# The residual gate of a mixture-of-experts block, multiplied into the expert rows while they leave PSUM

## The chip, the core and the metric

One core of one Trainium2 chip runs the whole program. The metric is the device time of one execution in microseconds (us); lower is better. Engines: TensorE (PE; its weight loads are PEld), VectorE (DVE), ScalarE (ACT), GpSimd (POOL) and SyncE (SP). SP and POOL issue nearly all DMAs here; POOL alone issues the indirect ones.

## The reference, cut to what matters

Two layers of a hybrid attention and mixture-of-experts model over 640 tokens of 1024 numbers: 128 prompt tokens and 512 latents. All values are 32-bit floats. Each layer ends so:

```
sh1, sc1, gt1, sh2, sc2, gt2 = modulation(cond, w_mod, b_mod)   # cond differs for prompt and latents
...
h2 = rms_norm(x, g_norm2) * (1 + sc2) + sh2
x = x + gt2 * moe(h2, w_router, b_router, w_gate, w_up, w_down)
```

In `moe` each token picks one group of experts and then its two best of the 16 experts, with weights w1 + w2 = 1:

```
for e in range(16):
    hid = silu(h @ w_gate[e]) * (h @ w_up[e])       # 256 wide
    out = out + combine[..., e:e + 1] * (hid @ w_down[e])
```

The gate gt2 is a row of 1024 numbers, one for the prompt tokens and one for the latents. The change is about where gt2 is multiplied.

## The kernel before

**Tiles of rows.** Tokens are held as five row tiles (NT = 5) of 128; tile 0 is the prompt. In the expert stage the 1280 pairs of token and expert are sorted into 18 expert tiles (MOE_TILES) of 128 slots. A "full" tile serves one expert, a "pair" tile two experts with 64 slots each. The order `SCHED` is: full, full, pair, full, pair, ... full, full, pair, so from tile 2 on the even tiles up to 14 are pairs, and tile 17 is one. Full tiles from tile 3 on are "split": their operands are cut into a high and a low part, and three matmuls take the place of one. ScalarE makes the high part (`moe_hi`), VectorE the low part (`moe_lo`, L1715; `x_lo`, L1720).

**One expert tile n.** POOL gathers the token rows (`rows`, L795) and, for a pair, the weights (`gu_a`, `gu_b`, `dn_a`, `dn_b`, L804 and L811); SP loads the weights of full tiles. TensorE, in this order within iteration n: `gate_up(n)` into PSUM bank 0, the transposes of the next tile's rows (L2197), `down(n - 1)` into banks 2 and 3, `hid_transposes(n)` (L2271). It goes on to `gate_up(n + 1)`, which waits for `hid(n)` on VectorE and, for a split tile, for `x_lo(n + 1)`. ScalarE does silu of one half of bank 0 (L1187), VectorE multiplies it with the other half into `hid` (L1758).

**The rows' way out.** `ys(n)` copies banks 2 and 3 out to `ysb[n % 2]`, a row of 1024 per slot, times the slot's weight `w_slot`: columns 0 to 511 on ScalarE (L1178), 512 to 1023 on VectorE (L1732). It waits for `down(n)` and, from tile 2 on, for the store of tile n - 2 from the same buffer (`y_stored`). Both engines do `ys(n - 1)` in iteration n, VectorE behind `hid(n)` and `x_lo(n + 1)`. POOL then scatters the row tile to `ye_d` in HBM (`store_rows`, L830). These stores stand in POOL's queue between the gathers of later tiles. `down(n)` on TensorE waits for `ys(n - 1)`.

**Rows of a layer put together.** When all stores have landed, SP loads for each row tile t the two rows of each token, `Y1[t]` and `Y2[t]`, two loads of 512 KB (`load_back`, L610). Before that, `rows_return` has loaded x (L598) and, behind its first tile, the gate as `gt` (two loads of 512 KB, broadcast over the partitions, L601). VectorE does three operations on 128x1024 per row tile, each behind the one before: Y1 += Y2 (`mix_rows`, L1357), Y1 *= gt (`gate_rows`, L1361), x += Y1 (`add_rows`, L1365). After layer 0 they are interleaved with the head of layer 1: square and root on ScalarE (L954, L958), scale (L962), transposes on TensorE (L1802), modulation shared by ScalarE (L968) and VectorE (`head_half`, L1337), high part on ScalarE (L972, L974). After layer 1 nothing but the three operations and the stores to `y_out` (L672) is left.

Of the kernel before, what the change touches and what calls it, by code (L numbers as in the profile page):

```python
# [137 lines left out]
def program(nc, w_stream, w_gu, w_dn, x_in, c_cols, params, b_mod2, vecs, g_norm2, da_kc, da_vc, na_kc, na_vc, na_bias,  # L138
# [3 lines left out]
    with ctx:  # L142
# [56 lines left out]
        tok = at("tok", [P, 2 * NT], F32)  # L199
        junk_off = top[0]  # L200
# [59 lines left out]
        ecmp = at("ecmp", [P, N_FULL + N_HALF, N_EXP], F32, 92)  # L260
        rc_f = at("rc_f", [P, NRC], F32, 92)
# [215 lines left out]
        y_act = Signal("y_act", MOE_TILES)  # L477
        y_dve = Signal("y_dve", MOE_TILES)
        y_stored = [Signal(f"y_stored{b}", half[b], 0, 16) for b in range(2)]
        gathered = [Signal(f"gathered{t}", 5 if t == 0 else 3, 0, 16) for t in range(NT)]  # L480
# [73 lines left out]
        def _(sp):  # L554
# [9 lines left out]
            for l in range(DEPTH):  # L564
# [26 lines left out]
                def rows_return(l):  # L591
# [4 lines left out]
                    sp.wait_ge(mod_stored.sem, mod_stored.at(l, 3))  # L596
                    for t in range(NT):
                        sp.dma_start(x[:, t, :], x_spill[:, t, :]).then_inc(gathered[t].sem, 16)  # L598
                        if t == 0:
                            for cond in range(2):  # L600
                                sp.dma_start(gt[:, cond, :], mod_d[l, cond, 5 * D:6 * D].partition_broadcast(P)  # L601
                                             ).then_inc(gathered[0].sem, 16)
# [39 lines left out]
                head_pair(3)  # L642

# [33 lines left out]
        def _(po):  # L677
# [17 lines left out]
            for l in range(DEPTH):  # L695
# [131 lines left out]
                def store_rows(n):  # L827
                    po.wait_ge(y_act.sem, y_act.at(l, n))
# [51 lines left out]
        def _(act):  # L880
# [4 lines left out]
            for l in range(DEPTH):  # L885
# [284 lines left out]
                def ys(n):  # L1170

                    act.wait_ge(*down_done(l, n))
                    if n >= 2:
                        act.wait_ge(y_stored[n % 2].sem, y_stored[n % 2].at(l, n // 2 - 1))
                    if n == 0:
                        act.wait_ge(ws_ready.sem, ws_ready.at(l, 0))
                    c = XD_COL[n]
                    act.activation(ysb[n % 2][:, 0:512], ps[:, 2, :], ACT.Copy, scale=w_slot[:, c:c + 1]).then_inc(y_act.sem, 1)  # L1178

                x_in_act(0)  # L1180
                for n in range(MOE_TILES):
# [10 lines left out]
                    if n >= 1:  # L1192
                        ys(n - 1)
# [8 lines left out]
                ys(MOE_TILES - 1)  # L1202
# [7 lines left out]
        def _(dve):  # L1210
# [9 lines left out]
            for l in range(DEPTH):  # L1220
# [134 lines left out]
                def mix_rows(l, t):  # L1355
                    dve.wait_ge(gathered[t].sem, gathered[t].at(l, gathered[t].n - 1))
                    after(chained(dve.tensor_tensor(Y1[t][:], Y1[t][:], Y2[t][:], ALU.add)))  # L1357

                def gate_rows(l, t):
                    mix_rows(l, t)  # L1360
                    return chained(dve.tensor_tensor(Y1[t][:], Y1[t][:], gt[:, GI(t), :], ALU.mult))  # L1361
# [26 lines left out]
                else:  # L1388
                    add_rows(0, gate_rows(l - 1, 0))
                    for t in range(NT):  # L1390
# [4 lines left out]
                        if t + 1 < NT:  # L1395
                            add_rows(t + 1, gate_rows(l - 1, t + 1))
# [327 lines left out]
                def ys(n):  # L1724

                    dve.wait_ge(*down_done(l, n))
# [5 lines left out]
                    dve.tensor_scalar(ysb[n % 2][:, 512:1024], ps[:, 3, :], w_slot[:, c:c + 1], None, ALU.mult).then_inc(y_dve.sem, 1)  # L1732
# [17 lines left out]
                if l + 1 < DEPTH:  # L1750
                    head_rows(l + 1)
                for n in range(MOE_TILES):
                    nxt = n + 1 if n + 1 < MOE_TILES else None
                    if nxt is not None and IS_SPLIT[nxt]:
                        for k in range(4):
                            moe_lo(SCHED[nxt][1], k)
                    dve.wait_ge(silu_done.sem, silu_done.at(l, n))
# [3 lines left out]
                    if n == 0:  # L1761
                        dve.wait_ge(ws_done.sem, ws_done.at(l, 0))
                        TS(row_i[:], ps[:, 4, 2 * MOE_TILES:3 * MOE_TILES], float(2 * NT * P), None, ALU.add)
                        TS(w_slot[:], ps[:, 4, MOE_TILES:2 * MOE_TILES], 1.0 / W_UNIT, None, ALU.mult).then_inc(ws_ready.sem, 1)
                    if IS_SPLIT[n]:
                        moe_lo(SCHED[n][1], 4)
                    if n >= 1:
                        ys(n - 1)
# [10 lines left out]
                ys(MOE_TILES - 1)  # L1779
# [3 lines left out]
                else:  # L1783
                    for t in range(NT):
                        add_rows(t, gate_rows(l, t))
# [617 lines left out]
```

## Time and profile before

| what | value |
| --- | --- |
| runs of the program | 1659.19 us median of 3 (1658.04 to 1663.81) |
| profiled execution | span 1665.8 us, from the first to the last instruction |
| TensorE matmul busy | 1550.5 us, 93% of the span |
| VectorE busy | 899.4 us, 54% |
| ScalarE busy | 700.1 us, 42% |
| GpSimd busy | 297.8 us, 18% |
| mean granted TensorE clock | 0.974 of full speed |
| expert stage of layer 0, first `hid` to last copy of rows | 629.4 to 826.7 us |
| expert stage of layer 1, the same | 1442.6 to 1636.5 us |

For the profiled execution the span is the time that is given; it is 6.6 us above the median of the runs. In the timelines a row gives the start, the duration, engine, line, operation, result and operands, how many instructions are merged, and in brackets how long the engine was idle before and what released it.

### The profile page before, as it was taken

The numbers are of one execution on the slowest core, as the hardware profiler recorded it, in microseconds if no ns is written. First come the engines' busy times: TensorE is split into PE (matmuls) and PEld (weight loads), VectorE is DVE, ScalarE is ACT, GpSimd is POOL, SyncE is SP. The second block draws the span as 40 slices with busy tenths as digits, with TensorE's granted clock in tenths as the row PEclk, the third lists the DMA queues.
The fourth block names the chain that finished last, engine by engine and source line by source line (L and its number), as shares of the span: only waits on it lengthen the run. The fifth ranks groups of instructions, "written<-read, shape, count | busy, mean of one in ns | idle before, by whom it ended". The sixth has DMA issues, their size and how long they took to land.

```text
span 1665.8 us, 21787 instructions
## 1 busy us (share of the span) xinstructions
PE 1550.5 (93%) x8180; PEld 1107.1 (66%) x8180; DVE 899.4 (54%) x1723; ACT 700.1 (42%) x1335; POOL 297.8 (18%) x321
## 2 busy tenths in 40 slices
PE   4999999999999989999779999999999999899992
PEld 1777777777787855554456777777777888555561
DVE  1566664455554752455575656543455556344554
ACT  4543554445521313444553455534454132144550
POOL 1001000011101014565200010000111010345640
PEclk9999999999999989999989999999999999999996
DMA  8541205534365379999847212353345253898847
GB/s 339 205 153 58 77 26 189 185 109 161 111 234 219 135 278 400 383 401 346 303 178 270 95 39 77 120 185 126 114 152 204 87 202 127 308 414 336 331 143 286
DMA packets 92376, 337.55 MB, mean 203 GB/s; under 512 B 20960, under 2 KB 21024, under 8 KB 89328
## 3 DMA queue, kind: packets, MB, share of 16 engines
q1 hardware_dynamic: 53136, 197.68, 32.5%
q0 software_dynamic: 38992, 135.86, 22.1%
q10 hardware_dynamic: 144, 2.62, 0.4%
q8 instruction: 65, 1.06, 0.3%
q14 instruction: 39, 0.32, 0.1%
HBM read 351.22 MB, written 47.35 MB: 239 GB/s over the span
## 4 chain that ended last, share of the span: by engine, by line
PE 81%; DMA 8%; DVE 6%; ACT 2%; issue 2%; SPq 1%; POOL 0%; POOLq 0%; ACTq 0%; DVEq 0%
PE ps L1884 16%; PE ps L1886 16%; PE ps L1885 16%; PE ps L2214 6%; PE ps L1876 5%; DMA gu_b<-w_gu,eidx 4%; PE ps L2263 3%; PE ps L2036 3%; PE ps L2018 2%; PE ps L1843 2%; PE ps L1792 2%; PE ps L2096 2%; PE ps L2197 2%; PE ps L2230 2%; PE ps L2070 1%
## 5 line engine op out<-in xcount | busy, mean ns | idle before, releaser
L1884 PE MATMUL ps<-hi,hT_hi 128*128 128x512 f32 x960 | 392.8, 409 | 5.5 <-ACT o_a L1094 3.0
L1886 PE MATMUL ps<-hi,hT_lo 128*128 128x512 f32 x960 | 377.1, 393 | 0.0
L1885 PE MATMUL ps<-lo,hT_hi 128*128 128x512 f32 x960 | 376.3, 392 | 0.0
L1884 PEld LDWEIGHTS ps<-hi,hT_hi 128*128 128x128 f32 x960 | 181.8, 189 | 64.8 <-issue 23.6
L1886 PEld LDWEIGHTS ps<-hi,hT_lo 128*128 128x128 f32 x960 | 181.4, 189 | 40.1
L1885 PEld LDWEIGHTS ps<-lo,hT_hi 128*128 128x128 f32 x960 | 182.2, 190 | 32.4
L890 ACT ACTIVATE hi<-raw 128x1024 fp32r<-128x1024 f32 x106 | 108.4, 1054 | 136.6 <-DMA raw<-w_stream 136.6
L1236 DVE TENSOR_TENSOR lo<-raw,hi 128x1024 fp32r<-128x1024 f32 x106 | 127.5, 1220 | 65.4 <-ACT hi L890 65.0
L1715 DVE TENSOR_TENSOR lo<-raw,hi 128x1024 fp32r<-128x1024 f32 x96 | 112.7, 1221 | 39.7 <-ACT hi L1161 33.9
L2214 PE MATMUL ps<-gu_a,xT 128*64 128x512 f32 x256 | 116.1, 607 | 6.7 <-DMA gu_b<-w_gu,eidx 6.7
L2214 PE MATMUL ps<-gu_b,xT 128*64 128x512 f32 x256 | 116.1, 607 | 0.0
L1161 ACT ACTIVATE hi<-raw 128x1024 fp32r<-128x1024 f32 x96 | 95.5, 1055 | 5.0 <-PE ps L1886 5.0
L1071 ACT ACTIVATE e_da<-ps,neg_m 128x640 f32<-128x640 f32 (+1 forms) x80 | 55.9, 704 | 73.2 <-DVE neg_m L1493 73.2
L2214 PEld LDWEIGHTS ps<-gu_a,xT 128*64 128x64 f32 x256 | 34.5, 140 | 74.7 <-issue 74.7
L1493 DVE TENSOR_REDUCE neg_m<-ps 128x1 f32<-128x640 f32 (+1 forms) x80 | 53.7, 712 | 54.3 <-PE ps L2025 38.4
L1758 DVE TENSOR_TENSOR hid<-ps,silu_g 128x256 f32<-128x256 f32 x36 | 15.3, 424 | 124.1 <-ACT silu_g L1187 107.0
L1351 DVE TENSOR_REDUCE ssum<-sq 128x8 f32<-128x512 f32 x40 | 27.4, 685 | 78.4 <-ACT stg L988 78.4
L1187 ACT ACTIVATE silu_g<-ps 128x256 f32<-128x256 f32 x36 | 13.8, 383 | 131.0 <-PE ps L1886 58.2
L987 ACT ACTIVATE sq<-ps 128x512 f32<-128x512 f32 x40 | 23.9, 597 | 104.5 <-PE ps L1886 104.5
L927 ACT ACTIVATE pT_na<-ps 128x384 f32<-128x384 f32 (+1 forms) x80 | 31.8, 446 | 77.0 <-PE ps L1876 77.0
L2263 PE MATMUL ps<-dn_a,hidT 128*64 128x512 f32 x128 | 60.0, 612 | 3.2 <-ACT hidT L1195 1.7
L830 POOL DMA_INDIRECT ye_d<-ysb,row_i x36 | 50.7, 1409 | 65.9 <-DVE ysb L1732 57.5
(312 smaller groups left out, 2880.8 us busy)
## 6 DMA issues: line engine op xcount, KB each, us to landing
raw<-w_stream SPq DMA_DIRECT2D x112, 512.0 KB
raw<-w_gu SPq DMA_DIRECT2D x80, 512.0 KB
raw_m<-w_stream SPq DMA_DIRECT2D x68, 512.0 KB, 5.4
raw<-w_dn SPq DMA_DIRECT2D x40, 512.0 KB
bias_na<-na_bias POOLq DMA_DIRECT2D x32, 384.0 KB, 3.4
sg<-sg_d POOLq DMA_DIRECT2D x8, 1280.0 KB, 9.7
y<-ye_d SPq DMA_DIRECT2D x20, 512.0 KB, 5.2
raw_p<-w_stream SPq DMA_DIRECT2D x16, 512.0 KB, 16.0
```

What stands on the lines that cost most here:

```text
L890: act.activation(hi[s][:], raw[s][:], ACT.Copy).then_inc(is_hi.sem, 1)
L1071: act.activation(e_da[:, i % 2, m, 0:nk], ps_flat[:, m * 1024:m * 1024 + nk], ACT.Exp, bias=neg_m[:, 2 * (i % 2) + m:2 * (i % 2) + m + 1], ...
L1161: act.activation(hi[k][:], raw[w][:], ACT.Copy).then_inc(is_hi.sem, 1)
L1236: dve.tensor_tensor(lo[s][:], raw[s][:], hi[s][:].bitcast(F32), ALU.subtract).then_inc(is_lo.sem, 1)
L1493: dve.tensor_reduce(neg_m[:, c:c + 1], ps_flat[:, m * 1024:m * 1024 + nk], AX.X, ALU.max, negate=True).then_inc(mx_done.sem, 1)
L1715: dve.tensor_tensor(lo[w][:], raw[w][:], hi[k][:].bitcast(F32), ALU.subtract).then_inc(is_lo.sem, 1)
L1876: ins = pe.transpose(ps[:, 5 + n % 2, j * P:(j + 1) * P], src, ident[:])
L1884: pe.matmul(out, w_hi, m_hi, start=first, stop=False)
L1885: pe.matmul(out, w_hi, m_lo, start=False, stop=False)
L1886: return pe.matmul(out, w_lo, m_hi, start=False, stop=last)
L2214: ins = pe.matmul(ps[cs, 0, :], xT[:, kc, cs], pair_gu[q % 2][h][:, kc * 512:(kc + 1) * 512], start=(kc == 0), stop=(kc == KC - 1))
L2263: ins = pe.matmul(ps[cs, 2 + c, :], hidT[:, k, cs], pair_dn[q % 2][h][k][:, c * 512:(c + 1) * 512], start=(k == 0), stop=(k == 1))
```

## The change

ScalarE's half of `ys` goes away. VectorE now does both halves, with the gate in them, and prepares the gate of each slot ahead.

- `gtm`, a new buffer of 8 KB per partition, gets both gate rows. SP loads them in each layer behind the last weights of the output projection, before it turns to the expert weights. The two loads of `gt` in `rows_return` go away. To make room, 8 KB instead of 16 KB of each partition are set aside for the descriptors of POOL's DMAs.
- Before the loop over expert tiles VectorE forms the difference of the two gate rows (prompt minus latents).
- `p_slot` is 1 for a slot that holds a prompt token and 0 for another, one small operation in iteration 0.
- `row_gates(n - 1)`: VectorE writes gate = difference * p_slot + latents' row (128x1024, from SBUF) into `ysb[(n - 1) % 2]`, in iteration n ahead of `hid(n)`. It carries the wait for the store of tile n - 3 from that buffer.
- `ys(n - 1)`: two operations of 128x512, PSUM * w_slot * gate in place.
- `gate_rows` goes away: two operations per row tile instead of three.
- The semaphore `y_act` goes away for POOL and TensorE.

```
+        gtm = at("gtm", [P, 2, D], F32)
...
+        p_slot = at("p_slot", [P, MOE_TILES], F32, 93.625)
...
-        gathered = [Signal(f"gathered{t}", 5 if t == 0 else 3, 0, 16) for t in range(NT)]
+        gathered = [Signal(f"gathered{t}", 3, 0, 16) for t in range(NT)]
...
                 def rows_return(l):
...
-                    sp.wait_ge(mod_stored.sem, mod_stored.at(l, 3))
                     for t in range(NT):
                         sp.dma_start(x[:, t, :], x_spill[:, t, :]).then_inc(gathered[t].sem, 16)
-                        if t == 0:
-                            for cond in range(2):
-                                sp.dma_start(gt[:, cond, :], mod_d[l, cond, 5 * D:6 * D].partition_broadcast(P)
-                                             ).then_inc(gathered[0].sem, 16)
...
                 head_pair(3)
+                sp.wait_ge(mod_stored.sem, mod_stored.at(l, 3))
+                for cond in range(2):
+                    sp.dma_start(gtm[:, cond, :], mod_d[l, cond, 5 * D:6 * D].partition_broadcast(P)
+                                 ).then_inc(gtm_loaded.sem, 16)
...
                 def store_rows(n):
-                    po.wait_ge(y_act.sem, y_act.at(l, n))
                     po.wait_ge(y_dve.sem, y_dve.at(l, n))
...
-                def ys(n):
-
-                    act.wait_ge(*down_done(l, n))
-                    if n >= 2:
-                        act.wait_ge(y_stored[n % 2].sem, y_stored[n % 2].at(l, n // 2 - 1))
-                    if n == 0:
-                        act.wait_ge(ws_ready.sem, ws_ready.at(l, 0))
-                    c = XD_COL[n]
-                    act.activation(ysb[n % 2][:, 0:512], ps[:, 2, :], ACT.Copy, scale=w_slot[:, c:c + 1]).then_inc(y_act.sem, 1)
...
-                def gate_rows(l, t):
-                    mix_rows(l, t)
-                    return chained(dve.tensor_tensor(Y1[t][:], Y1[t][:], gt[:, GI(t), :], ALU.mult))
...
-                def ys(n):
-
-                    dve.wait_ge(*down_done(l, n))
+                def row_gates(n):
+
                     if n >= 2:
                         dve.wait_ge(y_stored[n % 2].sem, y_stored[n % 2].at(l, n // 2 - 1))
                     if n == 0:
                         dve.wait_ge(ws_ready.sem, ws_ready.at(l, 0))
                     c = XD_COL[n]
-                    dve.tensor_scalar(ysb[n % 2][:, 512:1024], ps[:, 3, :], w_slot[:, c:c + 1], None, ALU.mult).then_inc(y_dve.sem, 1)
+                    return chained(STT(out=ysb[n % 2][:], in0=gtm[:, 0, :], scalar=p_slot[:, c:c + 1], in1=gtm[:, 1, :],
+                                       op0=ALU.mult, op1=ALU.add))
+
+                def ys(n, gated):
+
+                    dve.wait_ge(*down_done(l, n))
+                    after(gated)
+                    c = XD_COL[n]
+                    for j in range(2):
+                        half_row = ysb[n % 2][:, 512 * j:512 * j + 512]
+                        ins = STT(out=half_row, in0=ps[:, 2 + j, :], scalar=w_slot[:, c:c + 1], in1=half_row, op0=ALU.mult,
+                                  op1=ALU.mult)
+                    ins.then_inc(y_dve.sem, 1)
...
+                dve.wait_ge(gtm_loaded.sem, gtm_loaded.at(l, 1))
+                after(chained(TT(gtm[:, 0, :], gtm[:, 0, :], gtm[:, 1, :], ALU.subtract)))
                 for n in range(MOE_TILES):
                     nxt = n + 1 if n + 1 < MOE_TILES else None
                     if nxt is not None and IS_SPLIT[nxt]:
                         for k in range(4):
                             moe_lo(SCHED[nxt][1], k)
+                    if n >= 1:
+                        gated = row_gates(n - 1)
                     dve.wait_ge(silu_done.sem, silu_done.at(l, n))
                     dve.tensor_tensor(hid[:], ps[:, 0, D_EXP:2 * D_EXP], silu_g[:], ALU.mult).then_inc(hid_done.sem, 1)
...
+                        TS(p_slot[:], ps[:, 4, 0:MOE_TILES], P - NT * P - 0.5, None, ALU.is_lt)
...
-                        ys(n - 1)
+                        ys(n - 1, gated)
...
-                ys(MOE_TILES - 1)
+                ys(MOE_TILES - 1, row_gates(MOE_TILES - 1))
...
-                        pe.wait_ge(y_act.sem, y_act.at(l, n - 1))
                         pe.wait_ge(y_dve.sem, y_dve.at(l, n - 1))
...
-    nc = bacc.Bacc("TRN2", target_bir_lowering=False, num_devices=1)
+    nc = bacc.Bacc("TRN2", target_bir_lowering=False, num_devices=1, dynamic_dma_scratch_size=8192)
```

## Rows read from the trace of the kernel before

**Rows 1.** The page: span, and part 4, the chain that ended last.

```profile
span 1665.8 us, 21787 instructions
...
PE 81%; DMA 8%; DVE 6%; ACT 2%; issue 2%; SPq 1%; POOL 0%; POOLq 0%; ACTq 0%; DVEq 0%
```

**Rows 2.** Windows, layer 0: PE, PEld, DVE, ACT, POOL busy; clock, DMA share, GB/s.

```profile
680.00:700.00 20.00, 17.49 (x81) 8.41 (x80) 10.30 (x12) 9.56 (x14) 11.76 (x9) 0.91 0.93 376
...
740.00:760.00 20.00, 17.58 (x82) 10.99 (x82) 9.65 (x13) 10.53 (x16) 11.80 (x10) 0.91 1.02 416
```

**Rows 3.** Timeline, VectorE, layer 0: start, duration, instruction, [idle before].

```profile
672.50 0.42 DVE L1758 TENSOR_TENSOR hid<-ps,silu_g 128x256 f32<-128x256 f32 x1
673.29 1.29 DVE L1720 TENSOR_TENSOR xT_lo<-ps,xT_hi 128x512 fp32r<-128x512 f32 x2 [0.36 <-ACT xT_hi L1167]
678.73 0.75 DVE L1732 TENSOR_SCALAR ysb<-ps,w_slot 128x512 f32<-128x512 f32 x1 [4.16 <-DMA ye_d<-ysb,row_i]
...
743.98 0.75 DVE L1732 TENSOR_SCALAR ysb<-ps,w_slot 128x512 f32<-128x512 f32 x1 [1.28 <-DMA ye_d<-ysb,row_i]
```

**Rows 4.** Timeline, GpSimd, layer 0.

```profile
658.23 1.01 POOL L830 DMA_INDIRECT ye_d<-ysb,row_i  x1 [0.30 <-issue]
...
666.75 1.99 POOL L830 DMA_INDIRECT ye_d<-ysb,row_i  x1 [0.30 <-issue]
...
724.26 1.00 POOL L830 DMA_INDIRECT ye_d<-ysb,row_i  x1 [0.37 <-issue]
```

**Rows 5.** Timeline of TensorE, layer 0, tile 4.

```profile
675.83 0.48 PE L1884 MATMUL ps<-hi,xT_hi 128*128 128x512 f32 x1
```

**Rows 6.** The chain that ended last, layer 0: start, duration, what.

```profile
688.90 8.45 PE ps L2214 x32
...
711.76 7.02 PE ps L2214 x32
...
756.95 8.56 PE ps L2214 x32
```

**Rows 7.** Timeline of all engines, layer 1, tiles 4 to 6.

```profile
1488.57 0.48 PE L1884 MATMUL ps<-hi,xT_hi 128*128 128x512 f32 x1
...
1492.82 0.75 DVE L1732 TENSOR_SCALAR ysb<-ps,w_slot 128x512 f32<-128x512 f32 x1 [5.49 <-DMA ye_d<-ysb,row_i]
...
1497.27 1.09 PE L2263 MATMUL ps<-dn_a,hidT 128*64 128x512 f32 x1 [1.50 <-DMA dn_b<-w_dn,eidx]
...
1504.73 0.61 PE L2214 MATMUL ps<-gu_a,xT 128*64 128x512 f32 x1 [1.78 <-DMA gu_b<-w_gu,eidx]
```

**Rows 8.** Groups of VectorE by shape: busy us, mean ns of one | idle.

```profile
L1732 DVE TENSOR_SCALAR ysb<-ps,w_slot 128x512 f32<-128x512 f32 x36 | 27.0, 750 | 53.8 <-PE ps L2263 16.2 <-PE ps L1886 12.0 <-DMA ye_d<-ysb,row_i 10.9
...
L1578 DVE SCALAR_TENSOR_TENSOR mixed<-sg,ps 128x512 f32<-128x512 f32 x20 | 13.6, 687 | 18.9 <-PE ps L1886 18.9
...
L1278 DVE SCALAR_TENSOR_TENSOR G<-G,gn 128x1024 f32<-128x1024 f32 x4 | 4.7, 1219 | 0.0
```

**Rows 9.** Timeline of ScalarE between the layers.

```profile
846.91 0.63 ACT L974 ACTIVATE hT_hi<-y 128x512 fp32r<-128x512 f32 x1 [0.87 <-DVE y L1337]
...
854.80 0.63 ACT L974 ACTIVATE hT_hi<-y 128x512 fp32r<-128x512 f32 x1 [0.41 <-DVE y L1337]
```

**Rows 10.** Timeline of VectorE at the end of layer 0.

```profile
825.98 0.74 DVE L1732 TENSOR_SCALAR ysb<-ps,w_slot 128x512 f32<-128x512 f32 x1
```

**Rows 11.** The chain that ended last, end of layer 1.

```profile
1631.07 0.69 ACT ysb L1178
...
1639.92 4.46 DMA y<-ye_d
...
1645.66 1.24 DVE y L1361
...
1661.54 1.23 DVE x L1365
```

**Rows 12.** Busy time in the last stretches.

```profile
1641.00:1652.00 11.00, 0.00 (x0) 0.00 (x0) 7.46 (x7) 0.00 (x0) 0.00 (x0) 0.50 1.00 397
```

More of the change, by code:

```diff
@@ L476, in program @@
         ht_lo = Signal("ht_lo", sum(IS_SPLIT))
-        y_act = Signal("y_act", MOE_TILES)
+        gtm_loaded = Signal("gtm_loaded", 2, 0, 16)
         y_dve = Signal("y_dve", MOE_TILES)
         y_stored = [Signal(f"y_stored{b}", half[b], 0, 16) for b in range(2)]
-        gathered = [Signal(f"gathered{t}", 5 if t == 0 else 3, 0, 16) for t in range(NT)]
+        gathered = [Signal(f"gathered{t}", 3, 0, 16) for t in range(NT)]
         x_ready = Signal("x_ready", NT)
@@ L1191, in _ @@
                         moe_hi(SCHED[n][1], 4)
-                    if n >= 1:
-                        ys(n - 1)
                     act.wait_ge(ht_done.sem, ht_done.at(l, n))
@@ L1356, in mix_rows @@
                     dve.wait_ge(gathered[t].sem, gathered[t].at(l, gathered[t].n - 1))
-                    after(chained(dve.tensor_tensor(Y1[t][:], Y1[t][:], Y2[t][:], ALU.add)))
-                def gate_rows(l, t):
-                    mix_rows(l, t)
-                    return chained(dve.tensor_tensor(Y1[t][:], Y1[t][:], gt[:, GI(t), :], ALU.mult))
+                    return chained(dve.tensor_tensor(Y1[t][:], Y1[t][:], Y2[t][:], ALU.add))
                 def add_rows(t, n):
@@ L1388, in _ @@
                 else:
-                    add_rows(0, gate_rows(l - 1, 0))
+                    add_rows(0, mix_rows(l - 1, 0))
                     for t in range(NT):
@@ L1395, in _ @@
                         if t + 1 < NT:
-                            add_rows(t + 1, gate_rows(l - 1, t + 1))
+                            add_rows(t + 1, mix_rows(l - 1, t + 1))
                         head_half(t)
@@ L1767, in _ @@
                     if n >= 1:
-                        ys(n - 1)
+                        ys(n - 1, gated)
                     if n == 1 and l + 1 < DEPTH:
@@ L1778, in _ @@
                             next_lo(w)
-                ys(MOE_TILES - 1)
+                ys(MOE_TILES - 1, row_gates(MOE_TILES - 1))
                 if l + 1 < DEPTH:
@@ L1784, in _ @@
                     for t in range(NT):
-                        add_rows(t, gate_rows(l, t))
+                        add_rows(t, mix_rows(l, t))
         @blk.tensor
```

## The prediction

> **What bounds the kernel now.** I read the page first: 81% of the chain that ended last is TensorE, 8% are DMAs and 6% VectorE [rows 1]. Then the chain in order of time, for the places where VectorE or a DMA stands on it; then timelines of those places. The change touches three stretches. In the expert stage TensorE runs nearly without a gap, while the DMA engines are as full (share 0.93 and 1.02 in the two stretches shown). Twice in layer 0 TensorE stands still, 20 less 17.49 and 20 less 17.58 us, each time for a gathered weight tile, and the granted clock of that stretch falls to 0.91 [rows 2]. The reader is to see the price of such a stop: behind it the gate and up matmuls of a pair tile took 8.45 and 8.56 us, elsewhere 7.02 [rows 6]; the clock adds 1.4 us to the stop itself. Between the layers the chain runs through VectorE and ScalarE. At the end it is loads and VectorE alone [rows 11].
>
> **ScalarE's copies removed.** 36 of 0.69 us [rows 11]. ScalarE isn't what TensorE waits for inside the stage, so this is 0 there; in front of the last `down` of each layer the copy of tile 16 precedes the evacuation that `down(17)` waits for, which gives back up to 0.69 us.
>
> **VectorE's work per expert tile.** The gate of the slots is a 128x1024 operation of two SBUF operands; the nearest rows of that form took 1.22 us. The two halves go by the 128x512 operation with PSUM and SBUF operands, 0.69 us each, against 0.75 us for the half before [rows 8]. So VectorE works 1.22 + 2 x 0.69 - 0.75 = 1.85 us more per tile. The added 0.63 us of `ys` falls where `down(n)` is a whole `gate_up` away: 0. The gates come ahead of `hid(n)`, which TensorE needs soon. In full tiles VectorE idles some 5 us there: 0. In pair tiles it comes to `hid` without idling [rows 3], so `hid` and `x_lo` start up to 1.22 us later. `x_lo(5)` ended at 673.29 + 1.29 = 674.6, and `gate_up(5)` began at 675.83 [rows 5]: 1.25 us of cover, just enough, so 0; without it 1.2 us a pair tile. Tiles 15 and 16 are both split and TensorE has less beside them; I put 0.4 us in each layer, between 0 and 1.2.
>
> **The wait that moves.** This is the main cost. `ys(3)` stood 4.16 us for the store of tile 1, until 678.73 [rows 3]; POOL had issued it at 658.23, so it was out for 20.5 us [rows 4], behind the gathers. Before, `hid(4)` (672.50) and `x_lo(5)` were already done by then. Now `row_gates(3)` carries that wait and `hid(4)`, `x_lo(5)` are queued behind it, and TensorE waits for both. The chain: store landed 678.73, gates +1.22, `hid` +0.42, `x_lo` +1.29 = 681.7 against 675.83: TensorE stands 5.9 us. The clock takes 1.4 more. It would come to `gate_up(6)` at 688.90 - 2.51 + 5.9 + 1.4 = 693.7. The gathered tile had landed by 688.9, so the old stop is gone, and the matmuls end at 693.7 + 7.0 = 700.7 against 697.35: +3.35 us. At tile 12 TensorE would come at 756.95 - 2.42 + 3.35 = 757.9 to a tile that landed at 756.9, and end at 764.9 against 765.5. If the DMA engines, which are full there, deliver at the same time as before, the debt is paid (-0.6); if the gathers come as much later as they are issued, 3.35 us stay. A share of 1.02 speaks for the first; I take +0.5.
>
> In layer 1 the store of tile 1 held `ys(3)` for 5.49 us until 1492.82, and `gate_up(5)` had begun at 1488.57 [rows 7]. Now: 1492.82 + 1.22 + 0.42 + 1.29 = 1495.75, a stop of 7.2 us, with the clock 8.6. Given back: the waits of 1.50 us for `dn_b` and 1.78 us for `gu_b`, and the slow matmuls of 1.09 us behind the first (1.4 us). So `gate_up(6)` begins at 1504.73 - 1.78 - 1.50 - 1.4 + 8.6 = 1508.65 and ends at 1515.7 against 1511.75: +3.9 us. No later wait for weights is there to take it up. Bounds: 0 if the store should land early, 8.6 if nothing is given back.
>
> Other tiles: the store of tile 7, issued at 724.26 [rows 4], held `ys(9)` until 743.98 (19.7 us). `hid(10)` began at 743.98 - 1.28 - 1.29 - 0.36 - 0.42 = 740.6 [rows 3], with the debt of 3.35 us at 744.0; now at 745.2. The 1.2 us fit the cover. So a store may take 740.6 - 724.3 = 16.3 us from its issue before it delays `hid`.
>
> **The end of layer 0.** `ys(17)` began at 825.98 right behind other work of VectorE [rows 10], so its gates add 1.22 us and its halves 0.6; ScalarE's missing copy gives back 0.6: +1.2 us, at most 1.9.
>
> **Between the layers.** Five products of 1.24 us go (one is in [rows 11]). The first counts in full. Behind it, each round's end is ScalarE's L974, which had waited for VectorE's `head_half` for 0.87 us in the first round and 0.41 in the second [rows 9], 0.86 and 0.87 in the two others. When VectorE is 1.24 us earlier, ScalarE's own L972 and TensorE's transposes are late next, and only those gaps are won: 1.24 + 3.01 = 4.25 us. Bound: 6.2 if that chain moves too.
>
> **The last stretch.** Loads started landing at 1644.38 and x of tile 4 was done at 1661.54 + 1.23 = 1662.8 [rows 11]. With two operations per tile VectorE could be done at 1644.38 + 5 x 2.47 = 1656.7 (-6.1). But then the loads come next: ten of 512 KB are 5.24 MB, at 397 GB/s [rows 12] 13.2 us from 1641, so 1654.2, and 1.05 MB of the first two stores share the engines (+2.6): 1656.8, and 2.47 us for the last tile: 1659.3 (-3.5). I take -4.2. The copy of tile 17 costs nothing here: its gates fit beside `down(17)`, and 0.6 us more of `ys` stand against ScalarE's 0.69.
>
> **Loads of the gate.** In `rows_return` they were on no chain: 0. In layer 0 their new place falls into a stretch where the DMA engines idle: 0. In layer 1 they stand behind the last weight load of the projection, in the same queue: 0, up to 1.05 MB / 397 GB/s = 2.6 us. The difference and `p_slot` fall into idle time of VectorE: 0.
>
> **GpSimd.** The store at 658.23 took 1.01 us; that at 666.75, beside VectorE's two-operand operations, 1.99 [rows 4]. So VectorE's row work delays POOL. 18 gates in a layer overlap some issues; POOL idles between them. 0, at most 1 us for each of the four gathers that TensorE waited for.
>
> The Trainium skill (SBUF — State Buffer, Who interferes with whom) says that a VectorE instruction with two SBUF inputs contends with a GpSimd instruction that reads SBUF, and that the later one is blocked until the first ends. The two durations above agree; by the rule POOL would be held for up to 1.2 us per tile, by the rows' 1 us less than that, and either is hidden while POOL idles. The Trainium skill (TensorE: Matmul & The Clock Gate, Part 1: The HAM clock gate) says that TensorE's clock is halved by default and that activity releases it; the 8.45 us behind the stop agree, and without it my stops would be up to 2.8 us shorter.
>
> **The sum.** Expert stages +0.5 + 3.9 + 0.8, end of layer 0 +1.2, between the layers -4.25, last stretch -4.2: -2.05 us on a span of 1665.8. The span is 6.6 us above the median of the runs, 1659.2; the difference carries over: 1657.1 us.
>
> **Rivals.** *The waits are absorbed or never come* (0.19). The engines are near full either way, so a stop may only trade one wait for another. Expert stages -0.6 to +2, the rest -4.25 to -6.2, -3.5 to -6.1 and +1.2: -6 to -12, about 1650. Against it: the landing times of tile 1's stores are queue times that nothing here shortens.
> *Every pair tile waits for its store* (0.15). One mechanism: a store's way through the queue. It decides from 16.3 us on. At 20.5 us a pair tile's `hid` is 4.2 + 1.2 us late, less 1.25 of cover: 4.2 us of stop, with the clock 5.6. Four such tiles beyond the two counted give +22, so 1679; two give +11, 1668. For it: two stores of those shown took 19.7 and 20.5 us. Against it: a wait of `ys` for a store has come in two tiles only in layer 0 and one in layer 1, and each stop of TensorE empties the queue.
> *POOL falls behind* (0.05): blocked by VectorE's row work or by descriptor room that is half as large. +4 us for the four gathers, 1661. No row shows POOL waiting for room.
> My forecast has 0.61.
>
> **Chances and range.** 0.5% is 8.3 us; that is about what a measurement tells from no change. Faster by more: most of the first rival, 0.17. Slower by more: most of the second, 0.14. Within: 0.69. The range takes in the bounds (-11.7 with all low ends; +10 with all high ones, the unpaid debts and the load of gates in front), without the outermost: 1649.5 to 1668. The forecast's own is 1653 to 1662.
>
> **What the profile after would show.** In iteration 4 of each layer an idle time of TensorE of 5 to 8 us before `gate_up(5)`, with the matmuls behind it slow; `row_gates(3)` released by the DMA of `ye_d`; the stops before `gate_up(6)` and `gate_up(12)` shorter; L974 no longer released by VectorE; at the end VectorE waiting for `y` loads from the second or third tile on; x of tile 4 done some 4 us earlier relative to the first load. The prediction is wrong if stores land at other distances than 20 us in a full queue, if the debt of layer 0 isn't paid at tile 12, or if further pair tiles stop.

## The result and the profile after

The changed kernel takes 1668.52 us in the median of 10 runs (1666.37 to 1670.59); the kernel before took 1659.56 us in 10 runs beside it (1657.98 to 1667.54). The ratio is 1.0042, with a 95% interval of 1.003 to 1.0054: some 7 us slower (the two medians lie 9.0 us apart), inside the 0.5% that I had called no change. My 1657.1 us are 11.4 us too low, and the median lies 0.5 us outside my range.

The profiled execution took 1669.2 us, of which 1667.4 are span. The page's chain that ended last, by engine and by line, and the groups of VectorE on which the change works (busy us, mean ns | idle before and its releaser):

```profile
PE 82%; DMA 8%; DVE 5%; ACT 2%; issue 2%; SPq 1%; POOL 0%; POOLq 0%; ACTq 0%; DVEq 0%
PE ps L1883 17%; PE ps L1885 17%; PE ps L1884 17%; PE ps L1875 5%; PE ps L2213 5%; DMA ye_d<-ysb,row_i 5%; PE ps L2035 3%; PE ps L2017 2%; PE ps L2261 2%; PE ps L1791 2%; PE ps L1842 2%; PE ps L2095 2%; PE ps L2229 2%; PE ps L2196 1%; PE ps
...
L1724 DVE SCALAR_TENSOR_TENSOR ysb<-ps,w_slot,ysb 128x512 f32<-128x512 f32 x72 | 50.7, 745 | 34.1 <-PE ps L1885 11.6
L1714 DVE SCALAR_TENSOR_TENSOR ysb<-gtm,p_slot 128x1024 f32<-128x1024 f32 x36 | 46.0, 1279 | 36.6 <-DMA ye_d<-ysb,row_i 36.4
```

The stores of rows stand on the chain with 5%. `row_gates` (L1714) waits 36.4 us for them in all.

The chain around tile 4 of layer 0 shows how (start us, us, what):

```profile
656.06 0.99 POOL gu_a L805
657.05 0.30 issue
657.36 19.47 DMA ye_d<-ysb,row_i
676.83 0.03 issue
676.86 1.28 DVE ysb L1714
678.14 0.06 DVE hid L1756
678.20 0.19 issue
678.39 1.29 DVE xT_lo L1703 x2
```

This is the stop that I had foretold, answering to [rows 3]: the store of tile 1 stands behind the gathers, the gates behind the store, `hid(4)` and `x_lo(5)` behind the gates. TensorE's timeline beside it:

```profile
674.52 0.40 PE L1885 MATMUL ps<-hi,hidT_lo 128*128 128x512 f32 x1
678.53 0.69 PE L2269 MATMUL ps<-ident,hid 128*128 128x128 f32 x2 [3.61 <-DVE hid L1756]
679.72 0.79 PE L1883 MATMUL ps<-hi,xT_hi 128*128 128x512 f32 x1 [0.51 <-DVE xT_lo L1703]
680.32 0.63 PE L1884 MATMUL ps<-lo,xT_hi 128*128 128x512 f32 x1
...
685.42 0.40 PE L1884 MATMUL ps<-lo,xT_hi 128*128 128x512 f32 x1
```

`gate_up(5)` begins at 679.72, before at 675.83 [rows 5], and for 5 us its matmuls take 0.63 us instead of 0.40. The granted clock of these microseconds is 0.55 (windows of the changed kernel: PE, PEld, DVE, ACT, POOL busy; clock, DMA share, GB/s); in the kernel before it was 1.00 in the same window, in which nothing had stopped:

```profile
680.00:686.00 6.00, 6.00 (x16) 4.67 (x17) 2.27 (x3) 0.00 (x0) 2.58 (x2) 0.55 1.00 414
```

Counted from silu of tile 4 in each trace, `gate_up(5)` begins 4.8 us later than before, and from there to silu of tile 5 it takes 2.6 us longer: 7.5 us in all. In layer 1 the two parts are 4.8 and 1.6 us.

What I had not foretold stands in iteration 10, in VectorE's timeline, with GpSimd's for the store that it waits for:

```profile
740.48 2.35 DVE L1698 TENSOR_TENSOR lo<-raw,hi 128x1024 fp32r<-128x1024 f32 x2
746.38 1.28 DVE L1714 SCALAR_TENSOR_TENSOR ysb<-gtm,p_slot 128x1024 f32<-128x1024 f32 x1 [3.55 <-DMA ye_d<-ysb,row_i]
747.59 0.42 DVE L1756 TENSOR_TENSOR hid<-ps,silu_g 128x256 f32<-128x256 f32 x1
```

```profile
723.95 0.99 POOL L796 DMA_INDIRECT xg<-h_d,inv_i  x1 [0.30 <-issue]
725.25 0.99 POOL L805 DMA_INDIRECT gu_a<-w_gu,eidx  x1 [0.30 <-issue]
727.41 1.25 POOL L830 DMA_INDIRECT ye_d<-ysb,row_i  x1 [1.17 <-DVE ysb L1724]
```

In the kernel before that store was issued at 724.26 [rows 4]; it is now 3.15 us later. It lands at 746.36, 18.95 us after its issue, and in the kernel before it had landed by 743.98 at the latest [rows 3]. The same stop stands in layer 1 (issue 1540.77, gates 1558.88).

The last stretch answers to [rows 11] (VectorE's timeline):

```profile
1640.39 1.41 DVE L1724 SCALAR_TENSOR_TENSOR ysb<-ps,w_slot,ysb 128x512 f32<-128x512 f32 x2 [2.60 <-PE ps L2261]
1649.53 1.23 DVE L1344 TENSOR_TENSOR y<-y,y 128x1024 f32<-128x1024 f32 x1 [7.73 <-DMA y<-ye_d]
1650.80 1.22 DVE L1348 TENSOR_TENSOR x<-x,y 128x1024 f32<-128x1024 f32 x1
...
1660.75 1.23 DVE L1344 TENSOR_TENSOR y<-y,y 128x1024 f32<-128x1024 f32 x1 [1.10 <-DMA y<-ye_d]
1662.01 1.22 DVE L1348 TENSOR_TENSOR x<-x,y 128x1024 f32<-128x1024 f32 x1
```

**Stage by stage.** One trace of each kernel isn't enough: executions of one kernel differ by up to 12 us. So the table takes four executions of the kernel before (the one of the front, two more, and one with less descriptor room, which is the same work) and two of the changed one. "Silu 0 to 5" is the time from the start of silu of expert tile 0 (L1187, now L1177) to that of tile 5, and so on; the other bounds are the start of the first load of Y1 and the end of x of row tile 4; us.

| stage | before: four executions | mean | after: two | mean difference |
| --- | --- | --- | --- | --- |
| L0, silu 0 to 5 | 52.6, 52.6, 52.6, 52.6 | 52.6 | 60.1, 60.4 | +7.6 |
| silu 5 to 6 | 15.8, 14.1, 17.8, 17.6 | 16.3 | 11.9, 11.9 | -4.5 |
| silu 6 to 11 | 52.4, 52.7, 52.3, 52.3 | 52.4 | 56.7, 54.1 | +3.0 |
| silu 11 to 12 | 15.8, 12.5, 13.8, 16.0 | 14.5 | 11.9, 11.9 | -2.7 |
| silu 12 to 17 | 52.2, 52.5, 52.5, 52.2 | 52.3 | 52.8, 53.8 | +1.0 |
| silu 17 to first load of Y1 | 13.2, 13.2, 13.5, 13.4 | 13.3 | 15.0, 15.0 | +1.7 |
| to x of tile 4 | 41.6, 41.8, 42.6, 41.9 | 41.9 | 38.6, 38.9 | -3.2 |
| to silu 0 of L1 | 569.8, 566.5, 568.1, 569.8 | 568.5 | 568.1, 569.0 | 0.0 |
| L1, silu 0 to 5 | 52.1, 52.2, 52.2, 52.1 | 52.2 | 58.6, 60.7 | +7.5 |
| silu 5 to 6 | 17.5, 12.7, 14.6, 13.7 | 14.6 | 11.9, 11.9 | -2.8 |
| silu 6 to 11 | 52.3, 52.8, 52.4, 52.8 | 52.6 | 54.3, 53.9 | +1.6 |
| silu 11 to 17 | 64.0, 64.0, 64.0, 64.0 | 64.0 | 64.6, 64.7 | +0.6 |
| silu 17 to first load of Y1 | 11.4, 11.4, 11.4, 11.4 | 11.4 | 12.5, 12.5 | +1.1 |
| to x of tile 4 | 23.2, 23.2, 23.2, 23.2 | 23.2 | 18.5, 19.3 | -4.3 |
| to the end | 3.0, 3.0, 3.0, 3.0 | 3.0 | 4.2, 4.2 | +1.2 |

Ahead of silu 0 of layer 0 the means are equal (629.1), though the two executions of the changed kernel lie 2 us apart there. The sum is +7.8 us, near the +7 of the runs. Where nothing waits, silu 5 to 6 and silu 11 to 12 take 11.86 us; what lies above that in the kernel before is TensorE waiting for gathered weights and the low clock behind it. The first column is the execution of the front: its 17.5 us in layer 1 are 3 above the mean.

### The profile page after: what moved, and what is told of

It reads as the page before. It is cut to its first block, busy times and chain, and to the rows that moved or that the text cites. A ratio compares the mean times of both kernels' runs of the same rounds, so it can differ in the third digit from the quotient of the medians.

```text
span 1667.4 us, 21717 instructions
## 1 busy us (share of the span) xinstructions
PE 1552.5 (93%) x8180; PEld 1109.2 (67%) x8180; DVE 953.3 (57%) x1789; ACT 679.8 (41%) x1299; POOL 300.9 (18%) x321
## 4 chain that ended last, share of the span: by engine, by line
PE 82%; DMA 8%; DVE 5%; ACT 2%; issue 2%; SPq 1%; POOL 0%; POOLq 0%; ACTq 0%; DVEq 0%
PE ps L1883 17%; PE ps L1885 17%; PE ps L1884 17%; PE ps L1875 5%; PE ps L2213 5%; DMA ye_d<-ysb,row_i 5%; PE ps L2035 3%; PE ps L2017 2%; PE ps L2261 2%; PE ps L1791 2%; PE ps L1842 2%; PE ps L2095 2%; PE ps L2229 2%; PE ps L2196 1%; PE ps L2069 1%
## 5 line engine op out<-in xcount | busy, mean ns | idle before, releaser
L1177 ACT ACTIVATE silu_g<-ps 128x256 f32<-128x256 f32 x36 | 13.8, 384 | 148.2 <-PE ps L1885 80.8
L1724 DVE SCALAR_TENSOR_TENSOR ysb<-ps,w_slot,ysb 128x512 f32<-128x512 f32 x72 | 50.7, 745 | 34.1 <-PE ps L1885 11.6
L1714 DVE SCALAR_TENSOR_TENSOR ysb<-gtm,p_slot 128x1024 f32<-128x1024 f32 x36 | 46.0, 1279 | 36.6 <-DMA ye_d<-ysb,row_i 36.4
```

What stands on the lines that cost most here:

```text
L1724: ins = STT(out=half_row, in0=ps[:, 2 + j, :], scalar=w_slot[:, c:c + 1], in1=half_row, op0=ALU.mult, op1=ALU.mult)
```

## The experiments

All ratios are to the kernel before, in runs beside it on the same chip; the edits are against the changed kernel unless said. The stages come from each kernel's one trace.

**Less descriptor room alone** (kernel before).

```
-    nc = bacc.Bacc("TRN2", target_bir_lowering=False, num_devices=1)
+    nc = bacc.Bacc("TRN2", target_bir_lowering=False, num_devices=1, dynamic_dma_scratch_size=8192)
```

> The kernel before with one thing of the change: 8 KB instead of 16 KB of each partition for the descriptors of GpSimd's DMAs. My theory (the cost is the moved wait for the store): no change, within 1.5 us of the kernel before. Rival (descriptor room delays GpSimd's issues of gathers and stores): +3 us or more, and the issues of L795, L804, L811 and L830 longer or later. The profile is also a second look at the expert stage as it was: the stops before gate_up(6) and gate_up(12) of layer 0 were 2.5 us each; they should be there again, or the profiled execution of the kernel before was not typical and some of the 6.6 us between its span and the median lies in them.

Ratio 0.9997 (0.9976 to 1.0019). The room costs nothing that can be measured, and its stages are in the table: the stops for weights came again in layer 0, that of layer 1 was 13.7 instead of 17.5.

**The wait alone** (kernel before).

```
+                    if n >= 3:
+                        dve.wait_ge(y_stored[(n - 1) % 2].sem, y_stored[(n - 1) % 2].at(l, (n - 1) // 2 - 1))
                     dve.wait_ge(silu_done.sem, silu_done.at(l, n))
```

> The kernel before with nothing but a wait added: in iteration n, from 3 on, VectorE waits ahead of hid(n) for the store that ys(n - 1) waits for anyway. My theory: the stops before gate_up(5) and in tile 10 appear in both layers, each 1.2 us shorter than in the changed kernel since no gates stand between the landing and hid. Layer 0 +1.5 to +3, layer 1 +2 to +3.5: +4 to +6 us in all, 1664 to 1666. Rival (the wait costs nothing since the DMA engines are full either way): within 1 us of the kernel before.

Ratio 1.0036 (1.0017 to 1.0055): one wait moved ahead of `hid` costs 6 us by itself, without any gates. Its row of iteration 4 (VectorE's timeline):

```profile
671.50 1.22 DVE L1715 TENSOR_TENSOR lo<-raw,hi 128x1024 fp32r<-128x1024 f32 x1
677.80 0.42 DVE L1760 TENSOR_TENSOR hid<-ps,silu_g 128x256 f32<-128x256 f32 x1 [5.08 <-DMA ye_d<-ysb,row_i]
```

Silu 0 to 5 took 57.4 us in layer 0 and 55.5 in layer 1, silu 5 to 6 11.9 in both, and silu 6 to 11 52.9 and 56.1: at tile 10 only layer 1 lost time in this trace. The stops at tile 4 are 2.6 to 5.2 us shorter than in the changed kernel, more than the 1.2 that I had expected. The rival (the wait is free since the DMA engines are full) falls.

**Late gates.**

```
-                    if n >= 1:
-                        gated = row_gates(n - 1)
...
-                        ys(n - 1, gated)
+                        ys(n - 1, row_gates(n - 1))
```

> The changed kernel with row_gates(n - 1), its wait for the store with it, moved behind hid(n), x_lo(n + 1) and the fifth low part, directly ahead of ys(n - 1). All of VectorE's work stays the same. My theory: the stops before gate_up(5) (7 us) and behind tile 10 (4 us), which the trace of the changed kernel shows in both layers, vanish. Layer 0's expert stage then costs what it cost before (0 to +1), so does layer 1's; the ends of the expert stages keep +1.9 and +1.1, and between the layers and in the last stretch the 4.7 us of each are won: about -6 against the kernel before, 1653 to 1656 us. Rival 1 (VectorE's additional work, 1.9 us a tile, is what costs): nothing is won, 1667 to 1669. Rival 2 (the loads of the gate or the descriptor room): also 1667 to 1669.

Ratio 0.9963 (0.9943 to 0.9982), 1657.27 us beside 1661.92: 6 us faster than the kernel before. VectorE does the same work as in the changed kernel; the wait now holds nobody (its timeline):

```profile
674.17 0.41 DVE L1754 TENSOR_TENSOR hid<-ps,silu_g 128x256 f32<-128x256 f32 x1
674.88 1.29 DVE L1703 TENSOR_TENSOR xT_lo<-ps,xT_hi 128x512 fp32r<-128x512 f32 x2 [0.28 <-ACT xT_hi L1167]
680.18 1.28 DVE L1714 SCALAR_TENSOR_TENSOR ysb<-gtm,p_slot 128x1024 f32<-128x1024 f32 x1 [4.01 <-DMA ye_d<-ysb,row_i]
```

From silu 0 to 17 its layers took 186.8 and 183.5 us, between the 184.4 to 190.7 and 181.6 to 185.9 of the kernel before. So neither VectorE's added 1.9 us per tile nor the loads of the gate cost anything in the expert stages.

**Gates early, in a buffer of their own.**

```
+        gbuf = at("gbuf", [P, D], F32)
...
                 def row_gates(n):
-                    if n >= 2:
-                        dve.wait_ge(y_stored[n % 2].sem, y_stored[n % 2].at(l, n // 2 - 1))
...
+                    else:
+                        dve.wait_ge(y_dve.sem, y_dve.at(l, n - 1))
...
-                    return chained(STT(out=ysb[n % 2][:], in0=gtm[:, 0, :], scalar=p_slot[:, c:c + 1], in1=gtm[:, 1, :],
+                    return chained(STT(out=gbuf[:], in0=gtm[:, 0, :], scalar=p_slot[:, c:c + 1], in1=gtm[:, 1, :],
...
                 def ys(n, gated):
                     dve.wait_ge(*down_done(l, n))
+                    if n >= 2:
+                        dve.wait_ge(y_stored[n % 2].sem, y_stored[n % 2].at(l, n // 2 - 1))
```

`ys` reads `gbuf` as its third operand, and 4096 stands in place of 8192 for the descriptors.

> The changed kernel with the gates of the slots in a buffer of their own (4 KB), still computed ahead of hid(n); the wait for the store goes back to ys(n - 1). 4 KB for the descriptors of GpSimd's DMAs are left. My theory: as with the gates moved behind hid, -6 us against the kernel before, 1653 to 1656; the gates ahead of hid cost at most 0.1 us a pair tile more. If it lies over 2 us above the kernel with late gates, it is the 1.28 us of the gates ahead of hid that cost there. Rival (VectorE's additional work ahead of hid is what costs): 1665 or more.

Ratio 0.9988 (0.9966 to 1.001): 2 us faster than the kernel before, where I expected 6. By medians it lies 3.4 us above the kernel with late gates, over the 2 us from which on I wanted to charge the gates ahead of `hid` with it; but the intervals overlap, and the smaller descriptor room (4096) was not run by itself. Its stages had no stop at tiles 4 and 10 (52.6, 52.3, 52.1 and 52.7 us), which is what separates the theories. Only the last tiles show a price of the gates ahead of `hid`: silu 12 to 17 of layer 0 53.0 against 52.45 with late gates, silu 11 to 17 of layer 1 64.6 against 64.0.

**Two operations, nothing else** (kernel before; the product with the gate is left out).

```
                 def gate_rows(l, t):
-                    mix_rows(l, t)
-                    return chained(dve.tensor_tensor(Y1[t][:], Y1[t][:], gt[:, GI(t), :], ALU.mult))
+                    dve.wait_ge(gathered[t].sem, gathered[t].at(l, gathered[t].n - 1))
+                    return chained(dve.tensor_tensor(Y1[t][:], Y1[t][:], Y2[t][:], ALU.add))
```

> The kernel before with one part alone: the product with the gate after each layer is left out (so x gets the experts' sum without its gate), two operations per row tile instead of three. My theory, from the trace of the changed kernel: the head of layer 1 begins 4.2 to 4.7 us earlier behind the loads of Y1 and Y2, the last stretch is 3.4 us shorter between x of tile 0 and x of tile 4 and 1.2 us before it: -8.5 to -9.5 us in all, about 1651 to 1653. Rival 1 (loads are late next and take it up): -4 us or less. Rival 2 (the whole chain moves between the layers, 6.2 us): -11.

Ratio 0.996 (0.9941 to 0.9979): -6.6 us, below my -8.5 to -9.5. Behind layer 0, from the first load to x of tile 4, it took 38.7 us (-3.2, as the changed kernel), behind layer 1 19.1 (-4.1), but then 4.1 to the end instead of 3.0: the stores to `y_out` now pile up behind x.

**Stores first in GpSimd's queue** (the gates stay early).

```
                 for n in range(MOE_TILES):
+                    if n >= 2:
+                        store_rows(n - 2)
                     if n + 2 < MOE_TILES:
                         rows(n + 2)
...
-                    if n >= 2:
-                        store_rows(n - 2)
```

> The changed kernel with GpSimd's stores at the head of each iteration of its queue instead of behind the gathers: in iteration 3 the store of tile 1 goes ahead of four gathers of weights, in iteration 9 that of tile 7 ahead of one gather of rows and one of weights. The gates and their wait stay ahead of hid. My theory (a store takes 18 to 20 us because it stands behind gathers in one queue): the store of tile 1 lands before 665 us, the stop before gate_up(5) vanishes in both layers, that of tile 10 gets shorter or vanishes; the gathers come some 1.3 us later each. 1656 to 1662 us. Rival 1 (a store takes 18 to 20 us from its issue wherever it stands): it is issued some 7 us earlier and the stops still vanish, but 18 us lie between issue and landing. Rival 2 (the gathers are now late instead): 1666 or more, with idle time of TensorE before gate_up of pair tiles, released by gu_a or gu_b.

Ratio 1.0068 (1.0043 to 1.0093): 11 us slower than the kernel before and some 4 us slower than the changed kernel, whose interval this one overlaps. Rival 2 came true, though the mechanism at tile 4 was as I said. GpSimd's timeline, and then the chain (a piece of time each):

```profile
656.35 1.27 POOL L830 DMA_INDIRECT ye_d<-ysb,row_i  x1 [5.58 <-DVE ysb L1724]
657.93 1.01 POOL L796 DMA_INDIRECT xg<-h_d,inv_i  x1 [0.31 <-issue]
659.25 1.00 POOL L812 DMA_INDIRECT dn_a<-w_dn,eidx  x1 [0.31 <-issue]
...
689.65 1.62 POOL L830 DMA_INDIRECT ye_d<-ysb,row_i  x1 [6.55 <-DVE ysb L1724]
```

```profile
673.04 16.74 DMA gu_b<-w_gu,eidx
689.77 0.14 issue
689.91 8.78 PE ps L2213 x32
```

The store issued at 656.35 landed at 664.64: 8.3 us instead of 19.5, with the four gathers of weights behind it instead of ahead. The Trainium skill (DMA: Bandwidth & Descriptors, Two DMAs through the same engine are not ordered) says that within one queue of one DMA engine descriptors start in order; the two durations agree. The long landings had moved rather than gone: the stores of tiles 3 and 9 took 18.4 and 20.6 us here. Silu 0 to 5 was 52.6 us in layer 0 again. But GpSimd stood 5.6 and 6.6 us for `ys` with gathers queued behind the wait, and these were late: silu 5 to 6 took 17.5 and 18.4 us, silu 11 to 12 of layer 0 19.4, silu 11 to 17 of layer 1 71.7.

**Gates late at one tile only.** Two kernels, this one and the same with 10 in place of 4:

```
-                    if n >= 1:
+                    if n >= 1 and n != 4:
                         gated = row_gates(n - 1)
...
-                        ys(n - 1, gated)
+                        ys(n - 1, row_gates(n - 1) if n == 4 else gated)
```

> The changed kernel with the gates of tile 3 alone, and their wait, moved behind hid(4) and x_lo(5); all other gates stay ahead of hid. The prediction had a stop at tile 4 and none at tile 10. My theory now: the stop at tile 10 has its own cause, the store of tile 7, which lands 18 to 20 us after its issue whether or not tile 4 stopped. Expected: the 7.4 and 6.4 us at tile 4 vanish, the waits for gathered weights at tile 5 come back (15.8 us from silu(5) to silu(6) in layer 0 and 14.6 in layer 1, instead of 11.9), 2 to 5 us at tile 10 stay in both layers: about 2 us above the kernel before, 1662 to 1665. Rival (the stop at tile 10 follows from that at tile 4, which shifts the queue): silu(6) to silu(11) takes 52.4 us again, the time is that of the kernel with late gates, 1657.

Ratio 0.9991 (0.9976 to 1.0005). Without the stop at tile 4 the one at tile 10 is there all the same:

```profile
743.49 1.28 DVE L1714 SCALAR_TENSOR_TENSOR ysb<-gtm,p_slot 128x1024 f32<-128x1024 f32 x1 [2.83 <-DMA ye_d<-ysb,row_i]
744.70 0.41 DVE L1756 TENSOR_TENSOR hid<-ps,silu_g 128x256 f32<-128x256 f32 x1
```

Silu 6 to 11 took 56.1 and 54.3 us, silu 5 to 6 17.6 and 18.0. The stop at tile 10 has its own cause, and tile 4 carries most of the loss: 1.0042 without the edit, 0.9991 with it. I had put it 2 us above the kernel before; it came out level or up to 4 us below.

> The changed kernel with the gates of tile 9 alone, and their wait, moved behind hid(10) and x_lo(11). It is the kernel that the prediction's sum describes: a stop at tile 4, none at tile 10. If the step that the debt of layer 0 is paid at tile 12 holds, silu(11) to silu(12) takes some 12 us instead of the 12.5 to 16.0 of the kernel before, and silu(5) to silu(6) 11.9. Expected: 59.9, 11.9, 52.5 and 12.0 to 13.0 us in layer 0, 58.6, 11.9, 52.5 and 64.6 in layer 1; 4 to 6 us less than the changed kernel, 1663 to 1665. Rival (the wait at tile 12 stays, since the gathers are issued later by the debt): 13.5 to 15.8 us from silu(11) to silu(12), 1666 or more.

Ratio 1.0035 (1.002 to 1.0049): about 1 us less than the changed kernel and not told apart from it, so my 4 to 6 us are as good as refuted. In layer 1 it was near what I expected (57.7, 11.9, 52.3, 64.6). In layer 0 silu 11 to 12 took 13.2, and silu 12 to 17 54.2, since the stop came one pair tile later. From its chain:

```profile
749.75 18.80 DMA ye_d<-ysb,row_i
768.57 1.29 DVE ysb L1714
769.86 0.06 DVE hid L1756
770.11 1.29 DVE xT_lo L1703 x2
```

The store of tile 9 is out for 18.8 us and holds `hid(12)`. From silu 0 to 17 layer 0 takes 192.3 us, against 193.2 and 192.0 in the changed kernel.

**Late gates, and those of tile 17 ahead of the next layer's low parts.**

```
-                    if nxt is None and l + 1 < DEPTH:
-                        for w in range(3):
-                            next_lo(w)
                 ys(MOE_TILES - 1, row_gates(MOE_TILES - 1))
                 if l + 1 < DEPTH:
-                    for w in range(3, SLOTS):
+                    for w in range(SLOTS):
                         next_lo(w)
```

> The kernel with late gates, and in addition the gates and copies of tile 17 of layer 0 ahead of the three low parts of the next layer's first weights instead of behind them. My theory: the gates of tile 17 fall beside down(17), and the last copy of layer 0 ends 1.0 to 1.5 us earlier (10.7 us from silu(17) to the last copy become 9.4); the projection of layer 1 waits for no low part. About 1 us less than the kernel with late gates, 1653 to 1656 against about 1657. Rival (the low parts are needed at once): no gain or a loss of up to 2 us.

Ratio 0.9966 (0.9949 to 0.9982), 1657.51 us beside 1661.93. From silu 17 to the last copy 9.5 us instead of 10.7, as foretold; in the whole time 1 us is below what the runs can show. With late gates alone it is the best version found.

**Once more, both kernels.**

> The changed kernel, unchanged, for one more profiled execution. Expected: 59.9 to 60.2 us from silu(0) to silu(5) in layer 0 and 58.4 to 58.7 in layer 1, 11.86 from silu(5) to silu(6) in both, 54 to 57 from silu(6) to silu(11); span 1665 to 1669. If the stops move by more than 1 us from one execution to another, the stages of the changed kernel can't be compared to tenths.

> The kernel before, unchanged, for a third profiled execution. Expected: silu(0) to silu(5) 52.6 and 52.1 us as in all others; the two stretches with the gathered weights of layer 0 and the one of layer 1 together between 39 and 49 us, against 35.6 where nothing waits; span 1654 to 1666.

The changed kernel's span was 1672.1 us, above my 1665 to 1669. Silu 0 to 5 took 60.4 in layer 0 and 60.7 in layer 1, outside my 59.9 to 60.2 and 58.4 to 58.7: the length of a stop does move by 2 us, while the 11.86 us behind it came again. The kernel before had spans of 1663.4 here and of 1653.8 in the execution below; the three stretches with gathered weights took 46.2 and 39.3 us. The second was below what I expected, 12.7 us from silu 5 to 6 of layer 1 instead of 13.5 to 14.7 and a span of 1653.8 instead of 1656 to 1662.

> The kernel before, unchanged, for one more profiled execution of it. The one on which the prediction rests had a span of 1665.8 us, 8 us more than the median of runs less the 1.8 us that lie around the span. My theory: its extra time sat for 3 to 4 us in the wait for gathered weights at tile 5 of layer 1 (17.5 us from silu(5) to silu(6), against 13.7 and 14.7 in two kernels that have the same work there), which the change takes up anyway, and for 1 to 3 us in the stretches that no part of the change touches. Expected: 13.5 to 14.7 us there, a span of 1656 to 1662. Rival: 17.5 us there again, and the difference to the median is spread over all stages.

## Why the prediction was wrong

**Right.** The main cost was named, at its place and nearly in its size. For tile 4 I had worked out a stop of 5.9 + 1.4 = 7.3 us in layer 0 and 7.2 + 1.4 = 8.6 in layer 1; measured 7.6 and 7.5 (6.4 and 8.6 in the two executions). That the sum of layer 0 fits so well is partly luck: in the profiled execution the stop itself was 4.8 us, 1.1 less than I had, and the low clock behind it cost 2.6 us, 1.2 more. That the debt (the time by which TensorE is late) takes the place of the wait at tile 5 held too: 11.86 us from silu 5 to 6. Free were, as said, the descriptor room and the extra work in full tiles; the tiles 15 and 16 cost 0.6 us in each layer against my 0.4. GpSimd didn't fall behind: its stores' issues took 1.37 us in the mean, before 1.41, so VectorE's added row work didn't lengthen them. The last load is what x of tile 4 waits for.

**Wrong, by the terms of the sum** (predicted; measured as the difference of means):

| term | predicted | measured |
| --- | --- | --- |
| expert stage of layer 0, with the last pair | +0.9 | +4.4 |
| end of layer 0 | +1.2 | +1.7 |
| between the layers | -4.25 | -3.2 |
| expert stage of layer 1, with the last pair | +4.3 | +6.9 |
| last stretch | -4.2 | -2.0 |
| sum | -2.05 | +7.8 |

1. *"Other tiles"*, the term that I had put at 0, failed: +3.0 us in layer 0 and +1.6 in layer 1 from silu 6 to 11. I moved `hid(10)` back by the debt of 3.35 us, to 744.0, and left the landing of tile 7's store at 743.98, though the store is issued behind the same debt. Both move. What counts is the distance from issue to landing: 18.95 us in the changed kernel (18.1 in layer 1) and 18.9 with less descriptor room alone, where by my own working 16.3 were free. My 19.7 us were no landing: in the pair tiles 6 to 14 of both layers `ys` starts after 1.28 to 1.33 us of idling, six times of ten put down to `down` (L1886), so the 1.28 us at 743.98 [rows 3] read as the same wait, and the store had landed by then at the latest. Tiles 8 and 10 of layer 1 show it (VectorE's timeline of the kernel before):

```profile
1537.07 0.75 DVE L1732 TENSOR_SCALAR ysb<-ps,w_slot 128x512 f32<-128x512 f32 x1 [1.30 <-PE ps L1886]
...
1558.40 0.75 DVE L1732 TENSOR_SCALAR ysb<-ps,w_slot 128x512 f32<-128x512 f32 x1 [1.28 <-issue]
```

So a store of tile 7 that comes some 19 us after its issue delays nothing while `ys` waits for it, and stops TensorE once `hid` does. I had counted the tiles in which `ys` waited visibly, where the landing had to be set against `hid`. The rival "every pair tile waits for its store" was half right: tiles 4 and 10 in each layer, and tile 12 of layer 0 in two of the five traces with the early wait and the stores at their old place.

2. *"The debt of layer 0 is paid at tile 12"* failed too. Full payment would have been -3.95 us there, and the sum had -2.85 (3.35 less 0.5). The -2.7 of the table look like it, but they stand behind the stop at tile 10, which the sum didn't have. Where that stop was taken away (gates late at tile 10), silu 11 to 12 took 13.2 us, 1.4 less than the mean before, and the store of tile 9 then held `hid(12)`; layer 0 kept 4 us where the sum had 0.5. A stop of TensorE gives something back where gathered weights are late next, but it doesn't clear the stores behind it.

3. *The giving back in layer 1*, 4.7 us as I worked it out, was 2.8. The execution on which I built had 17.5 us from silu 5 to 6, the mean of four is 14.6. The sum was then set against the median of the runs, which doesn't hold that extra time, so it was taken off twice. A stop 1.1 us shorter than I had worked out for tile 4 made up for part of it.

4. *The last stretch.* I had the copies of tile 17 at nothing. `ysb` of tile 16 now ended at 1636.59 and `down(17)`, which waits for it, began at 1636.70, 0.5 us later behind silu of tile 17 than before, and the last two halves take 1.41 us where one of 0.75 stood: 1.1 us in all. And behind x of tile 4 the stores of `y_out` take 1.2 us more, which I hadn't looked at.

5. *Between the layers* 3.2 us were won instead of 4.25, in the kernel with two operations and nothing else as well. The starts of L954 tell which rounds fell short: they were 7.91, 7.89, 9.49 and 9.45 us apart and are now 6.93, 6.92, 9.65 and 9.77. The first two rounds gave 1.0 us each where I had 0.87 and 0.41; the last two, where I had 0.86 and 0.87, gave nothing. In these VectorE is held by ScalarE's work for the projection (its timeline, third round of the changed kernel), a wait that grew from 1.27 to 1.75 us here and from 1.24 to 2.52 in the next:

```profile
860.65 0.69 DVE L1338 TENSOR_REDUCE ssum<-sq 128x8 f32<-128x512 f32 x1 [1.75 <-ACT stg L988]
```

Shown by runs is that the wait moved ahead of `hid` costs 6 us by itself, and that the change wins 6 us when gates and wait stand behind `hid`; that tile 4 carries most of the loss; and that for the store of tile 1 it is its place in the queue that makes the 19 us. These 6 and 6 us leave about 0 where the changed kernel has +7. There the gates (1.28 us) also stand between the landing and `hid`, and the stops at tile 4 are longer (silu 0 to 5 60.1 and 58.6 us or more, 57.4 and 55.5 with the wait alone). That this makes up all of the 7 us is not shown. Of the time from one execution to the next, up to 12 us, the traces show where it lies (the three stretches with gathered weights, 39.3 to 49.1 us in all, and the one between the layers) and not what makes it. That the changed kernel's runs lie within 4.2 us, where those of the kernel before beside it spread over 9.6, fits the table, in which its stops replace these waits; it was not tested.

## What to carry to other kernels

An operation that is prepared ahead takes its waits with it: set the landing of what it waits for against the instruction that will stand behind it, tile by tile, and move both ends when a debt moves one. Place it behind everything that a fuller engine needs; here the same work on the same engine was some 13 us apart (ratios 1.0042 and 0.9963) by that place alone. And before a wait is counted as given back, look at more than one execution: its mean is what can be won.

## Not expected

- One scatter took 8.3 or 19.5 us from issue to landing, by its place among four gathers.
- With another stop just ahead, the stretch with the gathered weights took 11.86 us each time (11.85 to 11.88 in the changed kernel), where it varied from 12.5 to 17.8 in the kernel before.
- Moving stores ahead of gathers took the stops away at tiles 4 and 10 and still left the kernel some 4 us slower than the changed one, 11 us slower than the kernel before: GpSimd stood up to 6.6 us at a wait with the gathers behind it.
- A wait that is named after a DMA in one tile need not be its wait: the same 1.3 us stand in the tiles beside it, for `down`.
